# A two-block transformer on one core: cubic root step, reordered routing, spread gathers, and mixer B by seven quarter products

## The reference

```python
def mixer_b(h, w_in, conv_w, w_out):
    b_gate, c_gate, xt = jnp.split(h @ w_in, 3, axis=-1)
    u = c_gate * xt
    y = lax.conv_general_dilated(u, conv_w[:, None, :], window_strides=(1,), padding=((1, 1),), ...)
    return (b_gate * y) @ w_out
# both layers of the first block
h = h + mixer(rms_norm(h, norm1[i]))
h = h + square(relu(rms_norm(h, norm2[i]) @ w1)) @ w2
```

```python
inv_freq = 1.0 / (theta ** (jnp.arange(half, dtype=jnp.float32) / half))
scores = sigmoid(h2 @ router_w); biased = scores + router_b
g_sel = argmax(sum of the two largest of the 4 biased scores of each group)
_, idx = top_k(where(in_group, biased, -inf), 2)
y = sum over the two experts of gate * (silu(x @ w_gate[e]) * (x @ w_up[e])) @ w_down[e]
```

## Time and profile before

| | us |
|---|---|
| runs (median of 3) | 2132.88 |
| profiled execution, span from first to last instruction | 2131.9 |
| TensorE matmuls busy | 2014.4 |
| VectorE busy | 993.5 |
| ScalarE busy | 332.7 |
| HBM read | 622.86 MB, 293 GB/s over the span |

### The profile page before, as it was taken

One profiled execution on the slowest core, in us unless ns is written; L12 is line 12 of the kernel. 1 busy time (PEld: TensorE's weight loads), 2 busy tenths in 40 slices (PEclk: granted clock), 3 DMA queues, 4 the chain that ended last, 5 costly groups with the idle time before them and its releaser, 6 DMA issues.

```text
span 2131.9 us, 26296 instructions
## 1 busy us (share of the span) xinstructions
PE 2014.4 (94%) x10846; PEld 1352.5 (63%) x10846; DVE 993.5 (47%) x1960; ACT 332.7 (16%) x729; POOL 0.2 (0%) x4
## 2 busy tenths in 40 slices
PE   8999999999999999999999998888999999988888
PEld 5999988999888999757734333333657644333333
DVE  4888863888333788355432222222256522222212
ACT  1343431000000000123201000000314101000000
POOL 0000000000000000000000000000000000000000
PEclk9999999999999999999999999999999999999999
DMA  7333446688345589342789999999934699999997
GB/s 317 130 135 132 141 156 248 247 320 320 138 158 214 214 320 337 120 178 85 294 355 400 429 426 428 429 428 426 384 141 177 238 402 405 427 426 428 427 428 328
DMA packets 117873, 625.53 MB, mean 293 GB/s; under 512 B 5760, under 2 KB 8448, under 8 KB 85632
## 3 DMA queue, kind: packets, MB, share of 16 engines
q1 hardware_dynamic: 116752, 619.06, 72.8%
q10 hardware_dynamic: 1008, 4.87, 0.6%
HBM read 622.86 MB, written 1.05 MB: 293 GB/s over the span
## 4 chain that ended last, share of the span: by engine, by line
PE 74%; DMA 18%; DVE 5%; ACT 1%; issue 1%; SPq 0%; DVEq 0%
PE ps L2880 13%; PE ps L2271 10%; PE ps L2297 8%; PE ps L2354 7%; PE ps L2234 6%; PE ps L2918 6%; DMA ring<-in_w_up 5%; PE ps L2548 4%; DMA spare<-in_w_down 4%; DMA spare<-in_w_gate 4%; DMA spare<-in_w_up 4%; PE ps L2541 3%; PE ps L2720 2%; PE ps L2339 2%; DMA ring<-in_w_down 2%; PE ps L2427 1%
## 5 line engine op out<-in xcount | busy, mean ns | idle before, releaser
L2880 PE MATMUL ps<-ring,work_rows 128*64 128x512 f32 x1248 | 445.9, 604 | 28.8 <-DMA ring<-in_w_up 12.7
L2880 PE MATMUL ps<-arena,work_rows 128*64 128x512 f32 x584 | 262.9, 603 | 22.8 <-DMA ring<-in_w_up 10.9
L2880 PEld LDWEIGHTS ps<-ring,work_rows 128*64 128x64 f32 x1248 | 139.5, 139 | 225.4 <-issue 222.2
L2918 PE MATMUL ps<-ring,arena 128*64 128x512 f32 x608 | 214.0, 602 | 12.3 <-DMA ring<-in_w_down 5.4
L2271 PE MATMUL ps<-arena,ring 128*128 128x256 f32 x1024 | 224.7, 379 | 0.0
L2271 PEld LDWEIGHTS ps<-arena,ring 128*128 128x128 f32 x1024 | 192.6, 189 | 27.4
L2354 PE MATMUL ps<-ring,work_rows 128*128 128x192 f32 x840 | 147.7, 327 | 0.4 <-ACT arena L929 0.4
L2880 PEld LDWEIGHTS ps<-arena,work_rows 128*64 128x64 f32 x584 | 78.5, 138 | 95.8 <-issue 91.1
L2050 DVE TENSOR_SCALAR arena<-arena 128x512 f32<-128x512 f32 x32 | 13.7, 428 | 265.9 <-ACT arena L1227 265.9
L2354 PEld LDWEIGHTS ps<-ring,work_rows 128*128 128x128 f32 x840 | 136.0, 190 | 1.5 <-issue 0.6
L2918 PE MATMUL ps<-arena 128*64 128x512 f32 x288 | 127.2, 594 | 8.9 <-DMA ring<-in_w_down 6.7
(11 more groups left out here) (409 smaller groups left out, 2538.0 us busy)
## 6 DMA issues: line engine op xcount, KB each, us to landing
ring<-in_mlp_w SPq DMA_DIRECT2D x32, 2048.0 KB, 13.1
ring<-in_w_up SPq DMA_DIRECT2D x32, 2048.0 KB, 34.7
ring<-in_w_gate SPq DMA_DIRECT2D x28, 2048.0 KB, 34.9
arena<-in_w_mod SPq DMA_DIRECT2D x24, 2048.0 KB, 8.0
ring<-in_w_down SPq DMA_DIRECT2D x24, 2048.0 KB, 36.8
arena<-in_w_gate SPq DMA_DIRECT2D x20, 2048.0 KB, 26.8
ring<-in_a_wqkv SPq DMA_DIRECT2D x24, 1536.0 KB, 7.4
arena<-in_w_down SPq DMA_DIRECT2D x18, 2048.0 KB, 28.0
```

Of the source, the lines that this page charges most:

```text
L2880: e = te.matmul(bank(b)[SB * h:SB * h + SB], xs(k, col, SB), slabs.chunk(m + h, k), start=(k == 0), stop=(k == KD - 1), skip_group_check=True)
L2918: e = te.matmul(bank(6 + o)[SB * h:SB * h + SB], ueT[a][:, P * k + SB * h:P * k + SB * h + SB], slabs.tile(m + h).rearrange("p (k n) -> p ...
```

## The change

- **Root.** Three Newton rounds (nine steps) become one Newton round and one cubic round (seven steps), in every `rsqrt` and in the routing.
- **Folds.** For the first norm of the second block in layer 0, three of the four squared pairs are folded, and TensorE's `sums` adds the fourth straight from the squares, with two fillers between. `permute` moves behind the spread.
- **Mixer B.** The first input slab stays plain; the other five go by seven quarter products (`b_unit`), with weight sums (`b_weight_sums`), token sums (`b_token_sums`) and joins (`b_joined`) on VectorE and partial copies (`b_partials`) on ScalarE, in two alternating sets of PSUM banks. The spread comes after the second slab. The output projection takes chunks 0 to 3 of the mixer output for its first four blocks before it waits for the second half.
- **Routing.** ScalarE copies the logits. Group scores are the maximum of six pair sums. `first_best` compares and breaks ties in one step per token half, with an index table shifted to negative. The matmul that counts tokens per group goes to another bank and leaves the path; own rank is a multiply with reduction per half; the first picks are made straight from the rank. Fillers go from four to two and from two to one.
- **Gathers.** One piece in each of groups 1, 2 and 3. The next layer's scales and masks move behind group 3.
- **Table.** The rotary inverse frequencies are computed in double precision and rounded once.

```diff
-FILL = 4
+FILL = 2
...
-                    act.wait_ge(u_ready, s)
-                sc.activation(tmp_a, bank(0, 2), ACT.Copy).then_inc(c_copied, 1)
-                if s == 0:
-                    act.wait_ge(x_spread, 2)
...
+            def b_partials(q, out):
+
+                a, c, b = b_banks[q % 2]
+                for n, (e, src) in enumerate(((0, a), (2, c), (1, a), (3, a))):
+                    act.wait_ge(s_product, 4 * BY_SEVEN + 28 + 4 * q - 4 + n + 1)
+                    sc.activation(b_seven[q % 2][e], src, ACT.Copy).then_inc(s_copied, 1)
+                ring.wait_done(act, B_WIN + q)
+                if q == 3:
+                    act.wait_ge(u_ready, 1)
+                elif q == 4:
+                    act.wait_ge(y_ready, 1)
+                sc.activation(out[:, 2:4, 0:P], a, ACT.Copy).then_inc(s_joined, 1)
+            b_partials(1, conv_u)
+            act.wait_ge(x_spread, 2)
+            sc.activation(scale_b.rearrange("p n t -> p (n t)"), bank(7), ACT.Copy).then_inc(x_copied, 1)
+            b_partials(2, mixB[:, 0:4, :])
+            b_partials(3, tmp_a.rearrange("p (k t) -> p k t", k=4))
...
                 squares(lay * 2 + (FIRST_NORM + 1))
+                act.wait_ge(t_logits, lay + 1)
+                sc.activation(logits[0:E], bank(6)[0:E, 0:S], ACT.Copy).then_inc(t_copied, 1)
                 act.wait_ge(t_score, lay + 1)
                 sc.activation(route[:, 0:64], route[:, 0:64], ACT.Exp, scale=-1.0).then_inc(t_exp, 1)
...
+            own.step(ve.scalar_tensor_tensor(out=y, in0=t, scalar=1.5, in1=y, op0=ALU.add, op1=ALU.mult))
+
+        def cubic(y, t, x):
+
+            own.step(ve.tensor_tensor(t, y, y, ALU.mult))
+            own.step(ve.scalar_tensor_tensor(out=t, in0=t, scalar=CUBIC, in1=x, op0=ALU.mult, op1=ALU.mult))
+            own.step(ve.scalar_tensor_tensor(out=t, in0=t, scalar=-1.25 / CUBIC, in1=t, op0=ALU.add, op1=ALU.mult))
+            own.step(ve.scalar_tensor_tensor(out=y, in0=t, scalar=1.875, in1=y, op0=ALU.add, op1=ALU.mult))
 
...
+                elif p == 2:
                     fold(2 * l + 2, 1)
                     fold(2 * l + 2, 2)
             if gain is not None:
                 by_gain(2 * l + 2, 3, gain)
...
+            def b_weight_sums(q):
+
+                ring.wait_landed(dve, B_WIN + q)
+                if q >= 3:
+                    ring.wait_done(dve, B_WIN + q - 2)
+                w, t = wcols(B_WIN + q), b_sum[q % 2]
+                a11, a12, a21 = w[:, 0:4, 0:S], w[:, 4:8, 0:S], w[:, 0:4, S:2 * S]
+                own.step(ve.tensor_tensor(t[0], a21, w[:, 4:8, S:2 * S], ALU.add))
+                own.inc(ve.tensor_tensor(t[1], t[0], a11, ALU.subtract))
+                own.step(ve.tensor_tensor(a21, a11, a21, ALU.subtract))
+                own.step(ve.tensor_tensor(t[2], a12, t[1], ALU.subtract))
+                if q > 1:
+                    dve.sem_inc(s_summed, 1)
+
...
+            def b_joined(q, out):
+
+                a, c, b = b_banks[q % 2]
+                part = b_seven[q % 2]
+                ring.wait_done(dve, B_WIN + q)
+                dve.wait_ge(s_copied, 4 * BY_SEVEN + 28 + 4 * q)
+                own.inc(ve.tensor_tensor(out[:, 0:2, 0:P], b, part[0], ALU.add))
+                own.inc(ve.tensor_tensor(out[:, 0:2, P:S], c, part[1], ALU.add))
+                own.step(ve.tensor_tensor(out[:, 2:4, P:S], part[2], part[3], ALU.add))
+                dve.wait_ge(s_joined, BY_SEVEN + q)
+            b_weight_sums(1)
+            token_mean(2, 7)
+            b_token_sums()
+            dve.sem_inc(s_summed, 1)
             own.step(ve.reciprocal(tok_inv, tok_mean))
             rsqrt(tok_root, tok_t, tok_mean)
             diagonals(0, tok_inv, False)
             diagonals(NT, tok_root, True)
...
+            b_weight_sums(2)
             for s in range(2):
-                ring.wait_done(dve, B_WIN + 3 * s + 1)
+                if s:
+                    b_joined(3, tmp_a.rearrange("p (k t) -> p k t", k=4))
+                    dve.sem_inc(c_copied, 1)
+                    b_weight_sums(5)
+                b_joined(3 * s + 1, conv_u)
                 dve.wait_ge(c_copied, s + 1)
-                ve.tensor_tensor(conv_u.rearrange("p k t -> p (k t)"), tmp_a, bank(2, 2), ALU.mult).then_inc(u_ready, 1)
+                ve.tensor_tensor(conv_u.rearrange("p k t -> p (k t)"), tmp_a, conv_u.rearrange("p k t -> p (k t)"), ALU.mult
+                                 ).then_inc(u_ready, 1)
                 dve.wait_ge(u_ready, s + 1)
+                if s == 0:
+                    b_weight_sums(3)
...
+                b_joined(3 * s + 2, mixB[:, 4 * s:4 * s + 4, :])
+                ve.tensor_tensor(mixB[:, 4 * s:4 * s + 4, :], conv_y, mixB[:, 4 * s:4 * s + 4, :], ALU.mult
+                                 ).then_inc(y_ready, 1)
+                if s == 0:
+                    b_weight_sums(4)
             for p in range(4):
                 out_pair(p, 5 + p // 2 + 1, (B_WOUT, B_WOUT + 1))
...
-                newton(tok_root, tok_t, tok_mean, 1)
-                dve.wait_ge(t_logits, lay + 1)
-                ve.tensor_copy(logits[0:E], bank(6)[0:E, 0:S]).then_inc(t_copied, 1)
-                newton(tok_root, tok_t, tok_mean, 2)
+                newton(tok_root, tok_t, tok_mean)
+                cubic(tok_root, tok_t, tok_mean)
                 dve.sem_inc(x_root, 1)
-
-                iota32 = con2("iota32").unsqueeze(1).broadcast_to([P, NT, E])
...
-                own.step(ve.tensor_tensor(gsum, lo[:, :, 0], lo[:, :, 1], ALU.max))
-                own.step(ve.tensor_tensor(second_, second_, gsum, ALU.max))
-                own.step(ve.tensor_tensor(gsum, top, second_, ALU.add))
-
-                def first_best(values, out, iota, n, signal=None):
-
-                    own.step(ve.tensor_reduce(best, values, AX, ALU.max))
-                    own.step(ve.tensor_tensor(out, values, best.unsqueeze(2).broadcast_to([P, NT, n]), ALU.is_equal))
...
+                def first_best(values, out, iota, n, signal=None, among=None):
+
+                    own.step(ve.tensor_reduce(best, values if among is None else among, AX, ALU.max))
+                    for r in range(NT):
+                        e = ve.scalar_tensor_tensor(out=out[:, r, :], in0=values[:, r, :], scalar=best[:, r:r + 1], in1=iota,
+                                                    op0=ALU.is_equal, op1=ALU.mult)
+                        own.inc(e)
+                    own.settle()
                     own.step(ve.tensor_reduce(best, out, AX, ALU.min))
...
-                                          ALU.mult))
-                own.step(ve.tensor_reduce(rank_of, own_rank, AX, ALU.add))
+                           con2("iota8"), NG, t_mask, pairs.rearrange("p (r g) n -> p r (g n)", r=NT))
+
+                dve.wait_ge(t_ranks, lay * 2 + 1)
+                for r in range(NT):
+                    own.inc(ve.tensor_tensor_reduce(own_rank[:, r, :], bank(5)[:, NG * r:NG * r + NG], group_of[:, r, :],
+                                                    1.0, 0.0, ALU.mult, ALU.add, rank_of[:, r:r + 1]))
+                own.settle()
+                for r in range(NT):
+                    e = ve.scalar_tensor_tensor(out=sel[:, r, 0:2, :],
+                                                in0=con2("slotj")[:, 0:SB].unsqueeze(1).broadcast_to([P, 2, SB]),
+                                                scalar=rank_of[:, r:r + 1],
+                                                in1=group_of[:, r, 0:2].unsqueeze(2).broadcast_to([P, 2, SB]),
+                                                op0=ALU.is_equal, op1=ALU.mult)
+                e.then_inc(first_ready, 1)
                 for r in range(NT):
...
-                    group(home, g * GROUP_SLABS, g, g * SB, slot_gate[:, 2 * g:2 * g + 2], pieces=g == 1)
-                    if g == 1 and lay + 1 < DEPTH:
+                    group(home, g * GROUP_SLABS, g, g * SB, slot_gate[:, 2 * g:2 * g + 2], c=g if g < PIECES else 0)
+                    if g == MIDDLE - 1 and lay + 1 < DEPTH:
                         layer_scales(lay + 1, work.rearrange("p r e -> p (r e)"))
...
                     e = te.matmul(bank(b)[:, r:r + 1], tmp[:, S * h + P * r:S * h + P * r + P], com("ones")[:, 0:1],
-                                  start=(h == 0 and r == 0), stop=(h == 1), skip_group_check=True)
+                                  start=(h == 0 and r == 0), stop=(h == 1 and folds(n) == 3), skip_group_check=True)
+            if folds(n) < 3:
+                fill(2, 7)
+                pe.wait_ge(x_squared, 4 * n + 4)
+                for h in range(2):
+                    for r in range(NT):
+                        e = te.matmul(bank(b)[:, r:r + 1], tmp[:, 1536 + S * h + P * r:1536 + S * h + P * r + P],
+                                      com("ones")[:, 0:1], start=False, stop=(h == 1), skip_group_check=True)
...
+
+                slab, at = B_WIN + q, 4 * BY_SEVEN + 28 + 4 * q - 4
```

(72 more changed lines are left out.)

160 lines of the change are left out of this document (81 added, 79 removed).

## The result

The kernel after took 2106.06 us (median of 4 runs, 2105.78 to 2107.62) where the kernel before took 2132.89 in the same measurement: a ratio of 0.9867, 95% interval 0.9852 to 0.9883, or 26.8 us less. The profiled executions have spans of 2131.9 and 2104.3 us, 27.6 apart, and mean granted clocks of 0.990 and 0.991.

What follows compares the result with a forecast made beforehand. TensorE was taken to bound the kernel up to about 1229 us, transfers from there. Terms 8.2 + 2.4 + 0.4 + 2 x 1.9 + 3.0 + 2.7 = 20.5 us off 2132.9 gave 2112.4, range 2107 to 2121.

Steps and rivals of the forecast that it cites:

- norm, layer 1: First norm of the second block, layer 1: folds kept, two root steps less, 0.4 us (0 to 0.6).
- the half clock as a risk (0.14): Rival: fewer fillers idle TensorE; two or three more half-clock events in the chain, 1.7 us each, 2116 to 2118; chance 0.14.
- the loss of one stretch as a chance (0.08): Better than summed: layer 1's half-clock stretch goes too, 1.7 us, and starting idles; 2110; chance 0.08.
- Mixer B: Five slabs at 12.50 us, 6.8 us saved, and the 1.38 us output projection stall gone: 8.2 (3 to 8.5).
- The rival that VectorE becomes the bound: Mixer B: sums cannot run under the products, five units wait 6.4 us each, 32 lost, 2144; chance 0.04.
- the one that the change does less there: Mixer B rival: 112 shorter instructions cost as much as 64 because sums share slab memory; 2119; chance 0.04.
- First norm: Second block, layer 0: fewer folds and root steps, idle filled so the clock stays up; 2.4 us (1 to 2.8).
- Routing: Score to gather, each layer: shorter dependent chain, with independent VectorE operations overlapping; 1.9 us (1.0 to 2.3), counted twice.
- Spread gathers: Second expert group: missing DMA flow regained, from 360 and 365 GB/s; 3.0 and 2.7 us (0 to 3.2 each).
- Transfers decide further forward: Rival: loads after routing set the end, so routing and spreading give nothing; 11.0 us, 2121.9; chance 0.15.

Runs made afterwards that it cites:

- The root alone: Kernel before with the cubic round in place of two Newton rounds in every root, nothing else: 2130.80 us against 2136.81, ratio 0.9979.
- nine steps put back: Kernel after with three Newton rounds again in mixer A's root of 128 x 12 alone: 2112.28 us against 2109.73 for the kernel after.
- the idle time filled: Kernel before with three fillers between the moved permute and the first norm's sums: 2133.41 us against 2136.11, ratio 0.9991.
- the gathers alone: Kernel before with only the three gathers spread over groups 1, 2, 3 and layer scales moved behind group 3: 2128.24 us against 2136.81, ratio 0.9972.
- the three measurements of the whole: Kernel after, unchanged, against kernel before: 2106.06, 2109.73 and 2108.71 us; ratios 0.9867, 0.9884 and 0.9871.

## Why the prediction was right and where it failed

By stage, from the table, between the two profiled executions (of the 2.8 that the stage of the first norm lost, the attention behind it took back 0.2):

| term | said | found |
|---|---|---|
| mixer A | 0 | 2.4 |
| half clock in the first MLP | 0 | 1.6 |
| mixer B | 8.2 | 8.1 |
| first norm, layer 0 | 2.4 | 2.6 |
| routing, both layers | 3.8 | 3.7 |
| gathers and experts, layer 0 | 3.0 | 4.2 |
| norm, layer 1 | 0.4 | 0.4 |
| half clock at the turn, layer 1 | 0 | 1.6 |
| gathers and experts, layer 1 | 2.7 | 3.0 |
| sum | 20.5 | 27.6 |

- **The range.** By its own term bounds the sum is 6.0 to 22.9 us, which is 2110.0 to 2126.9, and not the 2108 to 2118 that the prediction wrote and then took into its 2107 to 2121. With the 2.4 of mixer A in the sum the forecast would have been 2110.0. Of the other 3.9 us down to 2106.06, two half-clock stretches are 3.2 in the profiled execution.
- **The step that failed: the root in mixer A was never costed.** The prediction named the change "in every `rsqrt`" and then followed only the norms and the routing. The root of 128 x 12 in `root_q` stands in VectorE's queue ahead of the weight sums and the join, and TensorE waited six times for that join, 5.2 us in all, as a line of the waits view of before already said. Two steps of 0.2 less six times is 2.4. The root alone gave 2.5, nine steps put back took 2.4. The remaining callers gave nothing: the attentions and the rest of the first block are as long with the root alone as before, once the stretch is taken out. The prediction answered "who waits for this?" for the changed code, not for every caller of the changed function.
- **Half clock.** The prediction had the half clock as a risk (0.14) and the loss of one stretch as a chance (0.08). In the traces two went beyond the one at the first norm, 3.2 of the 27.6. The one in the first MLP follows the length of mixer A. It was there in all six traces with the old length, 339.6 us less the stretches in it; in none of the five with 337.1; in both with 332.8; and not with 332.8 and 1.4 of fillers ahead. Code and wait at the place were the same in all fourteen. So this part of the gain came from the shift that the missed term made. The stretch at the layer 1 turn and the one in the second MLP varied between executions of one kernel; those are luck of the profiled execution, or at least no run shows what decides them. Without the turn's, the sum is 26.0, and the three measurements of the whole gave 26.8, 24.4 and 27.4.
- **Mixer B** held by its own steps: 12.50 a unit, 1.38 of stall gone, VectorE idle for 3 to 8 us before four of five joins. The rival that VectorE becomes the bound is out. So is the one that the change does less there.
- **First norm.** Right, and by the mechanism named: without the idle time the half clock was gone (the idle time filled), and the half-clock fillers, not the root, set the spread (the root alone gave 0.03). But five of the eight traces with the new form of this norm have a stretch at the start of the second MLP, near 675 us, that none with the old form but idle filled has: there the stage gives 1.2 (210.25 to 209.06) and not 2.8. The prediction priced the stretch that goes and not one that may come in its place.
- **Routing.** 1.84 a layer against 1.9. Between the starts in the rows of before and after: sums to score 3.76 to 2.98, 0.78 (said 0.7); group scores and maximum 1.34 to 0.89, 0.45 (0.5); compare to ranks 0.86 to 0.84, 0.02 (0.1); ranks to product 0.87 to 0.65, 0.22 (0.24); product to gather 1.42 to 1.04, 0.38 (0.4). Independent VectorE operations start 0.11 apart though they take 0.2, 1042.95 to 1043.18. The rule of the Trainium skill, "VectorE: DVE Perf Modes", section "The DRAIN you can't avoid", by which the next one does not start until the pipe is empty, would have given 1.5, and these operations do not follow it. The same paragraph adds that a next operation that is not held starts earlier, which the prediction left out and with which this case's trace agrees.
- **Spread gathers.** The mechanism was right (428 GB/s in the windows that had 360). The size, 3.0, looks small by 1.2 in layer 0, but part of that is scatter: the stage took 447.7 us on the mean of the five traces with the experts of before and 444.2 on that of the eight with spread gathers, 3.6 apart. Thinner losses beside the window are not the reason: before and with the gathers alone, 425 and 425 GB/s flow in the 50 us ahead of it and 426 and 428 in the 100 us behind it, 0.5 us at most. For both layers 5.7 was said, and 5.2 to 7.1 found alone.
- **Transfers decide further forward.** Out. With the gathers alone the first gather of layer 0 starts at 1063.86 and the experts take 443.7 us; with the whole change it starts at 1046.37 and they take 443.7 to 444.7. A start 17 us earlier is kept.
